# S5 outputs and lag kernels as dense 64x64 matmuls, z put back by channel through DRAM

## The reference, cut to what matters

```
x_t = lam_bar * x_(t-1) + b_bar u_t          y_t = Re(C x_t) + D u_t
z   = gelu(y);  a, g = split(z @ w_glu);     y_b = a * sigmoid(g)
```

## Time and profile before

| | us |
|---|---|
| three runs | 1554.12, 1552.75, 1553.02; median 1553.02 |
| the profiled execution | 1552.46, of it span 1550.6 |
| PE busy | 1539.1 (99%) |
| DVE, ACT, POOL busy | 1032.7, 664.1, 463.4 |
| groups L681, L683 (s5_outputs) | 12.7 + 9.9 |
| group L667 (chunk_inputs) | 9.7 |
| groups L599, L602 (lag_kernels) | 5.2 + 2.4 |
| mean granted TensorE clock | 0.999 |

### The profile page before, as it was taken

The page is one execution under the profiler, slowest core; times in us unless marked ns, Lnnn a source line. Parts: engine busy times, 40 slices in busy tenths (PEclk is TensorE's granted clock), DMA queues, the critical chain, the costliest instruction groups (busy, mean ns, idle before and its releaser), DMA issues.

```text
span 1550.6 us, 34501 instructions
## 1 busy us (share of the span) xinstructions
PE 1539.1 (99%) x12870; PEld 1522.0 (98%) x12870; DVE 1032.7 (67%) x1469; ACT 664.1 (43%) x874; POOL 463.4 (30%) x591
## 2 busy tenths in 40 slices
PE   8999999999999999999999999999999999999998
PEld 8999999999999999999999999999999999999998
DVE  7766788888576666557777777676777764444443
ACT  6334345445576634444333334343433333333332
POOL 8994468877332100221111111111111110001100
PEclk9999999999999999999999999999999999999999
DMA  8886566666766577556555555555555465555552
GB/s 268 242 200 185 145 209 190 188 195 180 234 194 205 167 192 233 167 162 220 173 156 168 162 162 162 162 162 162 165 159 175 150 226 172 174 175 175 169 176 89
DMA packets 292864, 281.17 MB, mean 181 GB/s; under 512 B 29808, under 2 KB 283504, under 8 KB 292640
## 3 DMA queue, kind: packets, MB, share of 16 engines
q1 hardware_dynamic: 277200, 255.94, 54.7%
q10 hardware_dynamic: 13568, 16.62, 3.4%
q0 software_dynamic: 2000, 7.27, 1.4%
HBM read 266.60 MB, written 13.16 MB: 180 GB/s over the span
## 4 chain that ended last, share of the span: by engine, by line
PE 98%; DMA 0%; DVE 0%; SPq 0%; ACT 0%; ACTq 0%; issue 0%
PE banks L544 31%; PE banks L546 31%; PE banks L545 31%; PE banks L554 1%; PE banks L667 1%; PE banks L681 1%; PE banks L703 0%; PE banks L744 0%; DMA raw<-in_w_in 0%; PE banks L716 0%; PE banks L599 0%; PE banks L683 0%; PE banks L626 0%; PE banks L757 0%; ACT whi L882 0%; DVE wlo L1230 0%
## 5 line engine op out<-in xcount | busy, mean ns | idle before, releaser
L1230 DVE TENSOR_TENSOR wlo<-raw,whi 128x1024 fp32r<-128x1024 f32 x443 | 564.0, 1287 | 280.8 <-ACT whi L882 274.0
L882 ACT ACTIVATE whi<-raw 128x1024 fp32r<-128x1024 f32 x443 | 461.6, 1050 | 540.5 <-PE banks L546 492.3
L545 PE MATMUL banks<-h_lo,whi 128*128 128x288 f32 x1408 | 416.4, 296 | 0.0
L546 PE MATMUL banks<-h_hi,wlo 128*128 128x288 f32 x1408 | 416.3, 296 | 0.0
L544 PE MATMUL banks<-h_hi,whi 128*128 128x288 f32 x1408 | 415.2, 295 | 0.0
L544 PE MATMUL banks<-hhi,whi 128*128 128x288 f32 (+1 forms) x912 | 271.7, 298 | 3.4 <-DVE hlo L1256 3.0
L545 PE MATMUL banks<-hlo,whi 128*128 128x288 f32 (+1 forms) x912 | 269.5, 295 | 0.0
L546 PE MATMUL banks<-hhi,wlo 128*128 128x288 f32 (+1 forms) x912 | 269.4, 295 | 0.0
L545 PEld LDWEIGHTS banks<-h_lo,whi 128*128 128x128 f32 x1408 | 265.0, 188 | 0.1
L546 PEld LDWEIGHTS banks<-h_hi,wlo 128*128 128x128 f32 x1408 | 264.7, 188 | 0.0
L544 PEld LDWEIGHTS banks<-h_hi,whi 128*128 128x128 f32 x1408 | 264.4, 188 | 0.1
(11 more groups left out here) (337 smaller groups left out, 2192.9 us busy)
## 6 DMA issues: line engine op xcount, KB each, us to landing
raw<-in_w_up SPq DMA_DIRECT2D x352, 256.0 KB, 3.4
raw<-in_w_in SPq DMA_DIRECT2D x223, 256.0 KB, 3.4
raw<-in_w_down SPq DMA_DIRECT2D x176, 256.0 KB, 3.0
raw<-in_w_glu SPq DMA_DIRECT2D x64, 256.0 KB, 3.4
raw<-in_w_out SPq DMA_DIRECT2D x64, 256.0 KB, 3.3
raw<-in_w_attn_proj SPq DMA_DIRECT2D x32, 256.0 KB, 3.9
scratch_gates<-gt ACTq DMA_DIRECT2D x16, 288.0 KB, 3.7
gbt<-scratch_gates POOLq DMA_DIRECT2D x8, 288.0 KB, 3.7
```

What stands on the lines that cost most here:

```text
L545: pe.matmul(out, h, xl[:, kt, :], start=False, stop=False)
L546: mm = pe.matmul(out, lo, xh[:, kt, :], start=False, stop=kt == nk - 1)
L882: act.activation(whi[:, s, :, 0:cols], raw[:, s, :, 0:cols], ACT.Copy).then_inc(hi_ready, 1)
L1230: dve.tensor_tensor(wlo[:, s, :, 0:cols], raw[:, s, :, 0:cols], whi[:, s, :, 0:cols], ALU.subtract).then_inc(lo_ready, 1)
```

## The change

The four steps and 16 channels of one group become the 64 columns of one matmul: `clam` and `tlag` lose their zero blocks, `s5_outputs` becomes twenty-four 64x64 matmuls of 72 columns, on (h = 0) and off (h = 1) the diagonal of the array, in two PSUM banks. Its output has steps by channels on the partitions, so GELU writes `zq`, SP puts it to DRAM (`z_out`, four DMAs) and reads it back by channel (`z_in`, four DMAs) into `zs`, whose tokens are then ordered by step; rounding and subtracting follow two turns later. The GLU stage reads its accumulators in that order and writes in token order. In a turn `lag_kernels` now stands ahead of `s5_outputs`. POOL joins three semaphores to one, makes two adds where it made four and drops the clearing of `clam`.

```
-    clam ... [P, 4, 2, LC + 1, 32]         +    clam ... [P, 4, 2, LC + 1, GC]
-    tlag = [P, LC, 4, 32]; tk = [P, P]     +    tlag = [P, 4, LC, GC]; tk = [P, LC, GC]
 lags_out:
-                for i in range(4):
-                    sp.dma_start(W["lag"][:, LC - 1:, i, :], tk[32 * i:32 * i + 32, :]...)
+                sp.dma_start(W["lag"][:, LC - 1:, :], tk[:, :, :])
 lags_in:
-                for n in range(2):        # 64 partitions, 2 KB runs
+                for i in range(4):        # 32 partitions, 256 B runs
+            def z_out(jt):
+                sp.wait_ge(sem("zq_ready"), jt + 1)
+                for m in range(2):
+                    for h in range(2):
+                        sp.dma_start(W["z"][jt, h, m ^ h].rearrange("c b i a -> b c (i a)"), zq[64 * m:64 * m + 64, 2 * h:2 * h + 2, :]...)
+            def z_in(jt):
+                sp.wait_ge(sem("z_out"), 64 * jt + 64)
+                if jt > 1: sp.wait_ge(sem("z_ready"), jt - 1)
+                for i in range(4):
+                    sp.dma_start(zs[jt % 2][32 * i:32 * i + 32, :]..., W["z"][jt, i // 2]...[i % 2])
 SP, gate stage: load(q); q == 1 and it > 1: z_in(it - 2); q == 5: lags_out; q == 6 and it: z_out(it - 1); q == 7: lags_in
 SP, GLU turn 0: load 0; z_in(6); keys_in(0); load 1; values_in(0); load 2; z_out(7); load 3; z_in(7); mask_in(0)
 s5_outputs:
-            for b in range(LC):
-                for step in range(3):
-                    for i in range(4):
-                        out = aux[32 * i:32 * i + 32, 2, b:T:LC]      # 128x32
+            for i in range(2):
+                for step in range(3):
+                    for h in range(2):
+                        for n in range(2):   # 64x64: rows 64n, columns 64(n ^ h), bank 2 + h
 PE, gates:
-                    small += (s5_outputs(it - 1), lag_kernels(it))
+                    small += (lag_kernels(it), s5_outputs(it - 1))
-            pe.wait_ge(sem("z_ready"), NUT - 1)
+            pe.wait_ge(sem("z_ready"), NUT // 2)       # 8 before the second chunk, as before
 ACT lags: also waits y_ready it.  ACT gelu writes zq only; z_high(jt) waits zs_in and rounds:
+   gates(it): hi 0, hi 1, z_high(it - 2), hi 2, ...;  after hi(C_GLU, 1): z_high(6);  GLU turn 0: hi 2, z_high(7), prompt_exp(0)
 DVE:
+   gates(it): lo 1, z_low(it - 2), ...;  after the last gate_evac: z_low(6);  GLU turn 0: prompt_max(0), lo 2, z_low(7), prompt_scale(0)
 GLU stage: glu_gate and glu_a read acc as "(b a)" and write "(a b)"
```

More of the change, by code:

```diff
@@ L149, in hybrid_decoder_step_kernel @@
     vtok = at("vtok", [P, 2, KV], F32, KT + 2304)
[L151 removed]
+    clam = [at(f"clam{i}", [P, 4, 2, LC + 1, GC], F32, GR + 12416 * i) for i in range(2)]
     lt = [at(f"lt{i}", [P, 4, 2, NST], F32, GR + 7424 + 2048 * i) for i in range(2)]
@@ L211, in hybrid_decoder_step_kernel @@
     rm = at("rm", [P, 4, NCH], F32, WK + 20736)
-    zs = at("zs", [P, T], F32, WK + 21888)
+    zs = [at(f"zs{i}", [P, T], F32, (WK + 21888, GR + 14976)[i]) for i in range(2)]
+    zq = at("zq", [P, 4, NCH], F32, GR + 2560)
     tq = [at(f"tq{i}", [P, 4, 8, 8], F32, WK + 4608 + 1024 * i) for i in range(4)]
@@ L437, in _ @@
                         tables_in(it + 2)
+                    if q == 1 and it > 1:
+                        z_in(it - 2)
                     if q == 5:
                         lags_out(it)
+                    if q == 6 and it:
+                        z_out(it - 1)
                     if q == 7:
@@ L473, in _ @@
                 if i == 0:
+                    z_in(NUT - 2)
                     keys_in(0)
@@ L482, in _ @@
                     load("w_glu", C_GLU + 4 * i, 2 + q, KCH * q, CW * i)
+                    if i == 0:
+                        (z_out, z_in)[q](NUT - 1)
                 if i == 0:
@@ L689, in gates @@
                 if it:
-                    small += (lambda: s5_outputs(it - 1), lambda: lag_kernels(it))
+                    small += (lambda: lag_kernels(it), lambda: s5_outputs(it - 1))
                 group(1, 6 + it, c, KD, hhi, hlo, before={0: small})
@@ L906, in newest_out @@
                     act.wait_ge(sem("y_ready"), it - 1)
[L907 to L910, removed]
+                act.activation(clam[it % 2][:, :, :, 0, :], cnat[:, :, 4 * it:4 * it + 4, :].rearrange("p c i h -> p i c h"), ACT.Copy).then_inc(sem("c0_ready"), 1)
             def lags(it):
@@ L1024, in gelu, with z_high @@
                 if jt:
[L1025 to L1028, removed]
+                    act.wait_ge(sem("z_out"), 64 * jt)
+                act.activation(zq[:, :, :].rearrange("p (h i) a -> p h (i a)", h=2), aux[:, 2:4, P:P + 2 * NCH], ACT.Gelu_apprx_tanh).then_inc(sem("zq_ready"), 1)
+            def z_high(jt):
+                act.wait_ge(sem("zs_in"), 64 * jt + 64)
+                act.activation(zhi[:, jt, :], zs[jt % 2][:, :], ACT.Copy).then_inc(sem("zhi_ready"), 1)
             def gates(it):
@@ L1034, in gates @@
                 hi(c, 1)
+                if it > 1:
+                    z_high(it - 2)
                 hi(c, 2)
@@ L1061, in _ @@
             hi(C_GLU, 1)
+            z_high(NUT - 2)
             store_gates(0, 7 + N_GATE, 4 * N_GATE - 2)
@@ L1108, in _ @@
                 hi(c, 2)
+                if i == 0:
+                    z_high(NUT - 1)
                 prompt_exp(i)
@@ L1490, in gates @@
                 lo(c, 1)
+                if it > 1:
+                    z_low(it - 2)
                 if first:
@@ L1537, in _ @@
             gate_evac(0, 6 + N_GATE, C_GLU)
+            z_low(NUT - 2)
             dve.wait_ge(sem("masks_ready"), 1)
@@ L1597, in _ @@
                 lo(c, 2)
+                if i == 0:
+                    z_low(NUT - 1)
                 prompt_scale(i)
@@ L1921, in output_powers @@
                 for c, op in ((0, ALU.add), (1, ALU.subtract)):
[L1922 to L1928, removed]
+                    pool.tensor_tensor(clam[it % 2][:, :, c, 1:LC + 1, :], wq[2 * c][:, :, :, :], wq[2 * c + 1][:, :, :, :], op).then_inc(sem("c_ready"), 1)
+                pool.wait_ge(sem("c_ready"), 2 * it + 2)
             newest_inputs()
```

92 lines of the change are left out of this document (48 added, 44 removed).

## The result

Six runs of the changed kernel have a median of 1559.8 us (1559.43 to 1560.5), six of the kernel before on the same chip 1553.74 (1552.75 to 1554.69). The ratio is 1.0039, 95% interval 1.0026 to 1.0052: the change costs 6 us. The prediction said 1547.8, and its range ended at 1552.8.

The account below looks back on a forecast made before the run. The prediction took PE to bound the kernel, busy 1539.1 of 1550.6 us. From 1552.46 it took 6.9 us of PE gain and added 1.7 of waits: 1547.3 profiled, 1547.8 as median, range 1545.2 to 1552.8.

Parts of the forecast that it names:

- What bounds the kernel: Whole kernel: PE, busy 1539.1 of 1550.6 us; other engines matter only where PE waits, near deadline only at GLU start.
- Outputs: s5_outputs on PE, each gate turn: four quarters side by side, 0.76 us instead of 1.57, 0.81 saved.
- lag products: Lag matmuls on PE in the gate stage: 64 columns instead of 128, 0.25 us instead of 0.43, 0.18 saved.
- shape change: Turns 1 to 7 on PE: one more change of tile shape from the new order, 0.15 us lost each.
- The rival with two quarters at a time: s5_outputs: only two 64x64 quarters run together, 0.04 us saved instead of 0.81; total 1553.2 us, chance 0.12.
- The gate turns outside PE: Gate stage: about 3 us more of SP issues a turn, nothing reaches PE; bound 0 to 0.5 us, taken 0.
- PSUM in stride: glu_a reading PSUM in stride takes between 0.76 and 1.6 us, ending before the next softmax; no cost taken.
- the cover: Gate turns: three-chunk load lead of 9.6 us, less landing, rounding and subtracting, leaves 3.9 us to hide z transfers.
- The last unit: GLU start: unit 7's z ready at 414.4 to 415.5; two PE waits together 1.1 to 2.1 us, 1.7 taken.
- The third rival: SP's queue sets the pace: long z issues delay weight chunks in gate turns and GLU start; 1557.1 us, chance 0.08.

Follow-up runs that it names:

- e3: Changed kernel with the loop over h outermost in s5_outputs, so only the two quarters of one h follow each other; median 1562.85 us.
- e8: Changed kernel with the last unit's eight z transfers issued by POOL, z_high(7) and z_low(7) ahead of rounding GLU chunk 2; median 1548.75 us.
- e10: e8 with one single-column Exp on ACT right behind z_high(7), to load the table early; median 1546.89 us.
- e9: Changed kernel with 60 matmuls that nobody reads put into PE's wait for the last unit's z; median 1562.49 us.
- e6: Changed kernel with 24 already met SP waits put right ahead of the y_prompt output transfers; median 1557.15 us.
- e1: Changed kernel without the last unit's z transfers, GLU reading unit 6's z instead (unit 7 wrong); median 1547.98 us.
- e4: Changed kernel with the last unit's z transfers, out and in, issued by ACT instead of SP; median 1550.41 us.
- e11: Changed kernel, all z transfers on SP, with z_out(7) moved ahead of values_in(0) and z_in(7) ahead of load 3; median 1554.88 us.
- e2: Changed kernel keeping the last unit's z transfers, but z_high(7) and z_low(7) read unit 6's z without waiting (unit 7 wrong); median 1553.88 us.
- e7: e4 with 12 already met SP waits put ahead of the GLU loads; median 1551.8 us.

## Why the prediction was wrong

- *What bounds the kernel.* Right: PE, and the GLU start as the one place with a near deadline.
- *Outputs, lag products, shape change.* Right. The head of a turn is 0.89 us shorter (0.84 forecast), the gates all together 7.6 (6.9 forecast; 0.3 of the difference is one turn of the kernel before that took 29.39 us instead of 29.1, the rest isn't placed). The quarters run side by side; e3 has the wider spacing and its 5.2 us. Of the 0.11 to 0.19 us for a change of shape the rows give only 0.11 and 0.13; no row gives 0.19. The rival with two quarters at a time is out.
- *The gate turns outside PE, and PSUM in stride, taken at 0.* Right for PE: it is busy for all 226.90 us of the gates, and `glu_a` takes 757 ns in stride as it did without. But the cover was nearly used up: SP's spare time from the last `lags_out` to load 2 went from 3.0 us to 0.5, and this is where the next step went wrong.
- *The last unit.* This step failed: "z ready at 414.4 to 415.5", waits of 1.7 us together, up to 3.5. The mechanism was the one named, and its places were right, but each size was low. Counted from the start of the last turn (378.77 before, 373.73 after), load 2 came 2.8 us later than forecast, since SP, out of spare time, passed on every longer issue. From the first issue of `z_out` to its last landing it took 6.3 us, not 3.5 (issued in 2.65, not 1.7, the last landing 4.5 after its issue began, not 2.1). `z_in` took 6.3, not 3.5 to 4.5 (2.56, and 4.3). So z was ready 7.1 to 8.2 us later than forecast. PE on its side came 0.9 earlier: the forecast took only the last outputs, 0.8, off 414.86 and left out the shorter head of the last turn. With the forecast's 0.3 to 1.4 this makes 8.3 to 10.5 us, against a wait of 9.3. The sizes came from rows of other transfers: L419's issue of 0.43 us and landing of 2.1. Those are 16 KB written in the middle of a turn. These are 36 KB in runs of 576 bytes out and 288 bytes back, with weights and cache pages in flight. Which of these differences made the landings long was not isolated; it is not the transfer's shape alone, for the same `z_in` landed in 2.2 us at the shortest, 3.0 in the median, and 4.3 here. The Trainium skill ("DMA: Bandwidth & Descriptors", Anatomy of one DMA) puts the fixed part of a transfer issued from GpSimd at about 2.0 us. On GpSimd's queue the trace has 2.3 to 3.6 (e8) and up to 5.2 (e10), so here it is no more than a floor.
- *The clock.* Not foreseen: 2.4 us for the chunk behind the wait; e9, where PE is busy in the wait, has it at 1.00.
- *The tail.* Not foreseen: 2.4 us, from a fetch of SP's instructions that came to lie among the last transfers. e6 takes it away with instructions that do nothing, and e1, e4 and e8 by having fewer.
- *The third rival,* SP's queue, came nearest in time (1557.1), and half of its reason holds, an SP out of spare time. But it put the loss into the gate turns as well, by rare issues of 1.75 us. The loss is at the end alone.

The sum by what was measured: 1552.5 - 7.6 + 9.3 + 2.4 + 2.4, and 0.9 for the late start, is 1559.9; the profiled execution took 1559.98. GLU's remaining 0.2 is not accounted for. Why the start is 0.9 later, and whether it is so in every execution, stays open.

## What to carry to other kernels

Price a round trip through DRAM at its last use, not its typical one. There it has no later turn as cover. Take the issue order of the queue, what it already carries, and landings under load, and look for an idle queue first (here POOL's: 11 us of 1560 against SP's, 2 of them in the tail). Count the spare time of the issuing engine before and after an edit, not only that of PE. A wait that looks affordable can cost more than its length once the clock falls, and adding or removing instructions can move a fetch into a place where it shows.

## What the runs showed of the hardware

- Clock: after PE idled 9.3, 8.1, 5.3 and 4.5 us (after, e6, e3, e11) its granted clock was 0.50 for the next five us or nearly (matmuls 0.24 us apart instead of 0.13). After 2.2, 2.5 and 3.0 us (e2, e4, e7) it stayed at 1.00. But in e9 it fell after an idle time of 1.95 us, and in e7's tail to 0.50 with PE busy throughout, so the length of the idle time alone doesn't decide.
- Instruction fetch: a hole of 2.9 us in SP's stream (2.6 of it behind the last thing it could wait for), with an instruction packet of q14 in it. The same work with 24 more waits was 2.65 us faster. PE's hole of 1.95 us in e9 looks alike and was not settled.
- Four 64x64 tiles run side by side, 16 to 17 ns a record (28 when the two quarters of one h follow each other, e3), also where two row halves write into one PSUM bank. The Trainium skill ("TensorEngine Tiling (Array Packing)", Gotcha 1: PSUM Pressure) excludes the latter; the trace does not agree. The two halves write different partitions of the bank there; whether that is the reason wasn't tried.
- A strided 36 KB transfer: in the median 0.54 us (`z_out`) and 0.62 us (`z_in`) to issue on SP, up to 1.4; about 0.6 on POOL. From 2.2 us (the shortest `z_in` of after) to 5.2 us (e10) to land.
